# Output projections with activations as stationary operand, and sums turned by VectorE and transfers

## The chip, the cores and the metric

One NeuronCore of one Trainium2 chip runs the whole program. The metric is the device time of one execution in microseconds. Engines are PE (TensorE), PEld (its weight loads), DVE (VectorE), ACT (ScalarE), POOL (GpSimd) and SP (SyncE, which issues nearly all transfers).

## The reference

The program is a trunk of two decoder layers over 256 tokens of width 2048, in float32:

```python
h = x
for i in range(2):
    xn = rms_norm(h, norm_mix[i])
    mix = hgrn2_mixer(...) if i == 0 else short_conv_mixer(...)   # each ends in "@ w_out", 2048 x 2048
    h = h + mix
    h = h + conv_glu_ffn(rms_norm(h, norm_ffn[i]), ffn_w_up[i], ffn_conv[i], ffn_w_down[i])
return rms_norm(h, final_norm)
# hgrn2_mixer:   out = (rms_norm(o, out_gain) * silu(g)) @ w_out
# conv_glu_ffn:  u = causal_dwconv(xn @ w_up, conv_w); gate, val = split(u); (silu(gate) * val) @ w_down
```

`w_up` is 2048 x 11264 and `w_down` 5632 x 2048. Weights are read once each, about 460 MB.

## The kernel before

**Precision.** Each float32 operand is split into a high part (rounded to the fast format fp32r) and a low part, and a product is high*high + high*low + low*high. ACT makes the high part of a weight chunk (`split` on ACT, L463), DVE the low part (`split` on DVE, L742), PE multiplies.

**Chunks, groups, phases.** A `Phase` is one projection: `n` turns of a loop, `groups` groups per turn, each 512 output columns, `cpg` chunks per group (8 where 2048 rows are summed, 22 for the down projections). A chunk is 512 KB of weights. Four chunks are in flight (`RING`): while PE works on chunk c, SP loads later ones, and ACT and DVE split chunk c + 4 as soon as PE has finished chunk c. All engines walk the same list of steps (group g, step kk) and hang their other work on steps: `ahead` before the split of that step, `pieces` after it. Each engine's queue is in order.

**Two forms of matmul.** In the feature-stationary form (`parts` = 2) the weights are the stationary operand and h^T comes out, features on partitions. A chunk is four 128-row tiles by 256 columns, two parts make the 512 columns, and chunks are run in pairs: 8 high matmuls of 512 columns for each (L1392, both halves of the activation side by side), then 8 low ones of 256 for each (L1402). ACT copies the low sums out of PSUM for a correction (L470), or DVE adds both halves. In the token-stationary form (`parts` = 1, "wide") the activations are stationary (`wide_tokens`, L1458 to L1460): 12 matmuls of 512 columns a chunk, two token blocks on partitions, so the sums must be turned to features on partitions. PSUM has two sets (`SETS`) of accumulators: a wide group holds one set, a part of the other form holds one. PE waits on `acc_free` for a set when it begins a group or part, and the release comes from whoever has read it.

**Turning.** In the up projections and the second mixer's input projection, DVE transposes blocks of 32 x 32 out of PSUM into `turned` (`turn_group`, L874), SP stores it to `crossing` in HBM at step `STORED_AT` and fetches it permuted into `moved` at `FETCHED_AT` (L346, L353), and DVE takes it from there at step `SCALED_AT` of the group after (`scaled_moved`, L885), times the norm's root `rs`. In the first down projection ACT copies the sums to SBUF (L640), PE turns them with eight 128 x 128 transposes into `side` (`turn_sums`, L1368) after the first chunk of the next group, and DVE adds them to h from there.

**Around the change.** `HGRN_OUT` and `SC_OUT` are the two output projections, two loop turns of two groups, feature-stationary. At the end of a group or part DVE adds the sums to h (`h_ready`), ACT makes the high part of the next normed input and the squares (`residual`), and DVE the low part and the sum of squares (`normed`). After them comes an up projection (`UP0`, `UP1`), whose first group needs a free set and chunks already split. The order of chunks in a group is written out in `Phase.steps`.

## Time and profile before

| | |
|---|---|
| time, median of 3 runs | 2300.13 us (2299.28 to 2300.26) |
| profiled execution, its time | 2299.77 us |
| its span, first to last instruction | 2297.9 us |
| busy: PE, DVE, ACT | 99%, 74%, 46% |
| first output projection, PE | 405.5 to 497.8 us |
| first down projection, PE | 977.0 to 1219.1 us |
| second output projection, PE | 1482.6 to 1571.7 us |

Matmuls overlap, so busy time of PE is not a sum of costs: what a matmul costs is the distance of its start from the next one's. A row of the timeline is its start, its length, the engine and line, output from inputs, the shape and how many were merged; in brackets is the idle time before it and what ended that.

### The profile page before, as it was taken

The page shows a single profiled execution, that of the slowest core. Times are in us where ns is not written, and L with a number is a line of the kernel's source. Part 1 is how long each engine was busy: PE and PEld are TensorE (multiplying, and loading weights), DVE is VectorE, ACT ScalarE, POOL GpSimd, SP SyncE. Part 2 cuts the span into 40 slices and gives each one's busy share as a digit, 9 for nine tenths or more (in the row PEclk, how much of TensorE's full clock was granted, in tenths as well). Part 3 has the DMA queues.
Part 4 walks back from the last instruction along what each step waited for, and adds up shares of the span by engine and source line. Part 5 has one row for each costly group of instructions (what it writes and reads, how often), then busy time and mean ns, then how long its engine had stood idle before and what let it go on. Part 6 is the DMA issues. An engine that isn't in the chain of part 4 may idle for free.

```text
span 2297.9 us, 33410 instructions
## 1 busy us (share of the span) xinstructions
PE 2285.5 (99%) x11110; PEld 1916.0 (83%) x11110; DVE 1694.5 (74%) x2132; ACT 1049.6 (46%) x1089; POOL 2.8 (0%) x9
## 2 busy tenths in 40 slices
PE   9999999999999999999999999999999999999998
PEld 8888888888888888888888888888888888888887
DVE  7979788877878888865556676766878878876544
ACT  7444444454444454444444333444444444444443
POOL 0000000000000000000000000000000000000000
PEclk9999999999999999999999999999999999999999
DMA  7555555558888888875667888666888888887664
GB/s 247 166 174 160 179 164 166 183 189 236 242 245 233 244 243 240 242 214 188 191 191 208 243 238 245 202 193 197 248 242 240 242 244 236 241 249 219 220 192 155
DMA packets 389733, 493.55 MB, mean 215 GB/s; under 512 B 18704, under 2 KB 223888, under 8 KB 389520
## 3 DMA queue, kind: packets, MB, share of 16 engines
q1 hardware_dynamic: 388640, 490.01, 71.9%
q10 hardware_dynamic: 1008, 2.43, 0.3%
q8 instruction: 52, 0.85, 0.2%
q14 instruction: 33, 0.27, 0.0%
HBM read 459.85 MB, written 30.41 MB: 213 GB/s over the span
## 4 chain that ended last, share of the span: by engine, by line
PE 89%; DVE 6%; issue 3%; DMA 1%; ACT 1%; DVEq 0%; SPq 0%; ACTq 0%
PE acc L1459 24%; PE acc L1458 24%; PE acc L1460 24%; PE acc L1392 11%; PE acc L1402 6%; DVE w_parts L742 1%; DVE a_diag L1062 1%; DVE fpre L1047 1%; DMA raw<-in_hgrn_w_in 1%; DVE kl L1029 1%; PE side L1563 0%; DVE ql L1023 0%; ACT w_parts L463 0%; DVE ta L778 0%; DVE ta L769 0%
## 5 line engine op out<-in xcount | busy, mean ns | idle before, releaser
L742 DVE TENSOR_TENSOR w_parts<-raw,w_parts 128x1024 fp32r<-128x1024 f32 x816 | 992.8, 1224 | 551.8 <-ACT w_parts L463 425.6
L463 ACT ACTIVATE w_parts<-raw 128x1024 fp32r<-128x1024 f32 x815 | 860.1, 1059 | 1061.0 <-PE acc L1460 827.7
L1458 PE MATMUL acc<-w_parts,xn 128*128 128x512 f32 x1728 | 673.3, 390 | 0.0
L1460 PE MATMUL acc<-w_parts,xn 128*128 128x512 f32 x1728 | 672.6, 389 | 0.0
L1459 PE MATMUL acc<-w_parts,xn 128*128 128x512 f32 x1728 | 672.6, 389 | 0.0
L1458 PEld LDWEIGHTS acc<-w_parts,xn 128*128 128x128 f32 x1728 | 324.4, 188 | 67.5
L1460 PEld LDWEIGHTS acc<-w_parts,xn 128*128 128x128 f32 x1728 | 324.4, 188 | 67.2
L1459 PEld LDWEIGHTS acc<-w_parts,xn 128*128 128x128 f32 x1728 | 324.4, 188 | 66.9
L1458 PE MATMUL acc<-w_parts,act 128*128 128x512 f32 x704 | 274.3, 390 | 0.0
L1460 PE MATMUL acc<-w_parts,act 128*128 128x512 f32 x704 | 274.0, 389 | 0.0
L1459 PE MATMUL acc<-w_parts,act 128*128 128x512 f32 x704 | 274.0, 389 | 0.0
L1392 PE MATMUL acc<-xn,w_parts 128*128 128x512 f32 x896 | 216.0, 392 | 1.8 <-DVE xn L798 0.8
L1392 PEld LDWEIGHTS acc<-xn,w_parts 128*128 128x128 f32 x896 | 164.5, 188 | 35.2 <-DVE xn L798 1.4
L1459 PEld LDWEIGHTS acc<-w_parts,act 128*128 128x128 f32 x704 | 132.2, 188 | 27.4
L1460 PEld LDWEIGHTS acc<-w_parts,act 128*128 128x128 f32 x704 | 132.2, 188 | 27.4
L1458 PEld LDWEIGHTS acc<-w_parts,act 128*128 128x128 f32 x704 | 132.2, 188 | 27.2
L1392 PE MATMUL acc<-act,w_parts 128*128 128x512 f32 x512 | 122.7, 392 | 0.0
L1402 PEld LDWEIGHTS acc<-xn,w_parts 128*128 128x128 f32 x896 | 114.3, 191 | 4.8 <-DVE w_parts L742 0.4
L1402 PE MATMUL acc<-xn,w_parts 128*128 128x256 f32 x896 | 118.3, 284 | 0.0
L1392 PEld LDWEIGHTS acc<-act,w_parts 128*128 128x128 f32 x512 | 94.1, 188 | 18.2
L898 DVE SCALAR_TENSOR_TENSOR tb<-pad,par,tb 128x256 f32<-128x256 f32 x200 | 83.3, 478 | 0.0
L874 DVE STREAM_TRANSPOSE turned<-acc 128x512 f32<-128x512 f32 x108 | 71.0, 695 | 9.1 <-DVE tb L896 3.8
(157 smaller groups left out, 1223.0 us busy)
## 6 DMA issues: line engine op xcount, KB each, us to landing
raw<-in_ffn_w_up SPq DMA_DIRECT2D x352, 512.0 KB, 4.4
raw<-in_ffn_w_down SPq DMA_DIRECT2D x176, 512.0 KB, 4.6
raw<-in_hgrn_w_in SPq DMA_DIRECT2D x127, 512.0 KB, 3.8
raw<-in_sc_w_in SPq DMA_DIRECT2D x96, 512.0 KB, 4.6
crossing<-turned SPq DMA_DIRECT2D x54, 512.0 KB, 3.8
moved<-crossing SPq DMA_DIRECT2D x216, 128.0 KB, 4.5
raw<-in_hgrn_w_out SPq DMA_DIRECT2D x32, 512.0 KB, 4.0
raw<-in_sc_w_out SPq DMA_DIRECT2D x32, 512.0 KB, 4.7
```

The lines of the kernel that those rows point to most:

```text
L463: nc.scalar.activation(w_parts[:, c % RING, :, 0, :], raw[:, c % RING], ACT.Copy).then_inc(hi_ready, 1)
L742: v.tensor_tensor(w_parts[:, c % RING, :, 1, :], raw[:, c % RING], w_parts[:, c % RING, :, 0, :].bitcast(F32), ALU.subtract).then_inc(lo_r ...
L874: o = v.transpose(turned[:, :, b, :], acc[:, a % SETS, b, :].rearrange("p (j q f) -> p q j f", q=4, f=QUARTER))
L898: o = v.scalar_tensor_tensor(out=dst[:, j, :], in0=src, scalar=w, in1=dst[:, j, :], op0=ALU.mult, op1=ALU.add)
L1029: o = v.tensor_tensor(k_to[:, :, :, b], keys(kh, b, n), keys(suf, b, n), ALU.mult)
L1047: mark(v.tensor_tensor(pre[:, :, 1], pre[:, :, 1], pre[:, :, 0, n - 1:n].to_broadcast(shape), ALU.mult))
L1062: o = v.copy_predicated(a_diag[:].rearrange("p j b (w z n) -> p j (b w) z n", z=2, n=n)[:, :, :, 1], mask[:, None].to_broadcast([P, TG, P ...
L1392: o = mm(to[:, j, :], w[:, q, 0, j * P:(j + 1) * P], src[:, k * KW + q, :, :].rearrange("p n t -> p (n t)"), start=begin and q == 0, stop= ...
L1402: o = mm(to[:, j, T:], w[:, q, 1, j * P:(j + 1) * P], src[:, k * KW + q, 0, :], start=False, stop=end and q == KW - 1, skip_group_check=True)
L1458: mm(bank, x_hi, hi, start=begin and q == 0, stop=False)
L1459: low = mm(bank, x_hi, lo, start=False, stop=False)
L1460: high = mm(bank, x_lo, hi, start=False, stop=end and q == KC - 1)
```

## The change

The output projections become two phases each: three wide groups in one loop turn (`HGRN_OUT`, `SC_OUT`), then one feature-stationary group (`HGRN_LAST`, `SC_OUT_LAST`) in which chunks of the two parts alternate. Sums of a wide group are turned by DVE at its last step, cross through HBM, and are added at step 4 of the next group; ACT makes high parts and squares at step 5, DVE the low parts at step 6 (`ADDED_AT`, `SQUARED_AT`, `NORMED_AT`). In the first down projection three of four groups take the same way, with `pad` and `tb` as buffers in place of `turned` and `moved`; the last is turned by PE as before. The first down projection's sums are stored in two transfers instead of one. Set numbers are counted over the whole program where they were counted per phase.

```diff
         if self.wide(g):
             order = [(0, k) for k in range(self.cpg)]
-        elif first and g == 0 and self is HGRN_OUT:
-            order = [(0, 0), (0, 1), (1, 0), (1, 1), (0, 2), (1, 2), (0, 3), (1, 3)]
+        elif self.groups == 1:
+            order = [(0, 0), (1, 0), (0, 1), (1, 1), (0, 2), (1, 2), (0, 3), (1, 3)]
...
-HGRN_OUT = Phase(HGRN_IN, 2, 2, DT)
-UP0 = Phase(HGRN_OUT, 11, 2, DT, scales=2, corrects=False, parts=1)
+HGRN_OUT = Phase(HGRN_IN, 1, 3, DT, scales=3, corrects=False, parts=1)
+HGRN_LAST = Phase(HGRN_OUT, 1, 1, DT)
+UP0 = Phase(HGRN_LAST, 11, 2, DT, scales=2, corrects=False, parts=1)
 DOWN0 = Phase(UP0, 2, 2, FT, corrects=False, parts=1)
 SC_IN = Phase(DOWN0, 1, 10, DT, scales=10, corrects=False, parts=1)
 SC_LAST = Phase(SC_IN, 1, 2, DT, scales=2)
-SC_OUT = Phase(SC_LAST, 2, 2, DT, corrects=False)
-UP1 = Phase(SC_OUT, 11, 2, DT, scales=2, corrects=False, parts=1)
+SC_OUT = Phase(SC_LAST, 1, 3, DT, corrects=False, parts=1)
+SC_OUT_LAST = Phase(SC_OUT, 1, 1, DT, corrects=False)
+UP1 = Phase(SC_OUT_LAST, 11, 2, DT, scales=2, corrects=False, parts=1)
...
+ADDED_AT, SQUARED_AT, NORMED_AT = 4, 5, 6
...
+        turned_sums = pad[:, :, TAPS - 1:].rearrange("p q (b n) -> p q b n", b=T // P)
+        moved_sums = tb[:].rearrange("p j t -> p (j t)").rearrange("p (b a n) -> p b a n", b=T // P, a=4)
...
+            def fetch(to):
+
                 for q in range(4):
...
-                    sp.dma_start(moved[q * QUARTER:(q + 1) * QUARTER].rearrange("f b a n -> f (b a) n"),
+                    sp.dma_start(to[q * QUARTER:(q + 1) * QUARTER].rearrange("f b a n -> f (b a) n"),
                                  crossing[q].rearrange("b (a f) n -> f (b a) n", f=QUARTER)).then_inc(moved_in, 16)
+
+            def cross_sums(n, kk):
+
+                if n and kk == STORED_AT:
+                    sp.wait_ge(turned_ready, turned_groups[DOWN0] + n)
+                    for b in range(T // P):
+                        sp.dma_start(crossing[:, b].rearrange("q p n -> p q n"), turned_sums[:, :, b]) \
+                            .then_inc(sums_stored, 16)
+                if n and kk == FETCHED_AT:
+                    sp.wait_ge(sums_stored, 16 * (T // P) * n)
+                    fetch(moved_sums)
...
+            def cross_next(phase, g, kk):
+
+                if kk == STORED_AT and 0 < g <= phase.groups:
+                    store_turned(0, phase, g - 1)
+                if kk == FETCHED_AT - phase.cpg and 1 < g <= phase.groups + 1:
+                    fetch_moved(0, phase, g - 2)
...
+            stream(HGRN_OUT, hgrn_w_out[0], lambda i, g: g * GC, lambda i, first, g, kk: cross_next(HGRN_OUT, g, kk))
+            stream(HGRN_LAST, hgrn_w_out[0], lambda i, g: 3 * GC, lambda i, first, g, kk: cross_next(HGRN_OUT, 3 + g, kk))
...
+            def residual_phase(phase, last, r0, weight, rs_n=None, carry=None):
+
+                def behind(g, step):
+                    if g >= 0 and step == SQUARED_AT:
+                        for part in range(TG // TW):
+                            residual(0, r0 + g * (TG // TW), part, g * TG, weight)
...
+                def last_pieces(i, first, g, kk):
+                    behind(phase.groups - 1, kk)
+                    part, _, _, ends = last.steps(first, g)[kk]
+                    parts = range(last.parts) if rs_n is not None and kk == last.cpg - 1 else \
+                        [part] if rs_n is None and ends else []
+                    for part in parts:
+                        residual(0, r0 + phase.groups * last.parts, part, phase.groups * TG, weight)
...
-                if kk == 0 and n:
+                if kk == SQUARED_AT and n:
                     turned_residual(n - 1)
-                if kk != DOWN0.cpg - 1:
+                if (n, kk) != (DT // TG - 1, DOWN0.cpg - 1):
...
+            def add_moved(phase, g, tile, src):
+
+                dve.wait_ge(moved_in, (turned_groups[phase] + g + 1) * 4 * 16)
+                dst = h[:, tile:tile + TG, :].rearrange("p j (s t) -> p s j t", t=QUARTER)
+                v.tensor_tensor(dst, dst, src.rearrange("p b a (j t) -> p (b a) j t", j=TG), ALU.add).then_inc(h_ready, 2)
...
+                def behind(g, step):
+                    if g < 0:
+                        return
+                    tile, r, sq = g * TG, r0 + g * (TG // TW), sq0 + g * (TG // TW)
+                    if step == ADDED_AT and rs_n is not None:
+                        u = pad[:, :, TAPS - 1:]
+                        scaled_moved(0, phase, g, u)
+                        await_scaled(0, phase, g)
+                        for part in range(TG // TW):
+                            dst = h[:, tile + part * TW:tile + (part + 1) * TW, :]
+                            v.tensor_tensor(dst, dst, u[:, part * TW:(part + 1) * TW, :], ALU.add).then_inc(h_ready, 1)
+                    elif step == ADDED_AT:
+                        add_moved(phase, g, tile, moved[:])
+                    if step == NORMED_AT:
+                        dve.wait_ge(h_ready, r + TG // TW)
+                        for part in range(TG // TW):
+                            normed(0, phase, r, sq, part, tile, weight)
...
+                def turns(i, first, g, kk):
+                    if ahead:
+                        ahead(i, first, g, kk)
+                    if kk == phase.cpg - 1:
+                        turn_group(i, phase, g, turned[:])
...
+                    behind(g - 1, kk)
...
+                def last_pieces(i, first, g, kk):
+                    behind(phase.groups - 1, kk)
+                    part, _, _, ends = last.steps(first, g)[kk]
+                    tile = phase.groups * TG
...
-                        dve.wait_ge(lo_used, at(i, phase.cpi, c + 1 + RING))
+                        a = last.a0 + part
+                        c = last.c0 + kk
+                        dst = h[:, tile + part * TW:tile + (part + 1) * TW, :]
+                        dve.wait_ge(lo_used, c + 1 + RING)
                         link(v.tensor_tensor(dst, dst, acc[:, a % SETS, :, 0:T], ALU.add), i)
                         v.tensor_tensor(dst, dst, acc[:, a % SETS, :, T:], ALU.add).then_inc(h_ready, 1)
-                        dve.wait_ge(h_ready, at(i, 4, r + part + 1))
+                        dve.wait_ge(h_ready, r + part + 1)
                         v.sem_inc(acc_free, 1)
-                        normed(i, phase, r, sq, part, tile, weight)
-                phase_of(phase, pieces, ahead=ahead, into=lambda g: tb)
-
-            def turn_group(i, phase, g):
+                        normed(i, last, r, sq, part, tile, weight)
+                phase_of(phase, pieces, ahead=turns)
+                phase_of(last, last_pieces, into=lambda g: tb)
...
-                    turned_residual(n - 1)
-            phase_of(DOWN0, down)
+                r = 8 + (n - 1) * (TG // TW)
+                if n and kk == ADDED_AT:
+                    add_moved(DOWN0, n - 1, (n - 1) * TG, moved_sums)
+                if n and kk == NORMED_AT:
+                    dve.wait_ge(h_ready, r + TG // TW)
+                    for part in range(TG // TW):
+                        normed(0, DOWN0, r, r + 8, part, (n - 1) * TG, NORM_MIX + DT)
+
+            def turn_down(i, first, g, kk):
+                n = i * DOWN0.groups + g
+                if kk == DOWN0.cpg - 1 and n < DT // TG - 1:
+                    turn_group(0, DOWN0, n, turned_sums)
+            phase_of(DOWN0, down, ahead=turn_down)
...
+            phase_of(HGRN_LAST, act, act_ready, 0)
...
-            def turn_down(i, first, g, kk):
-                n = i * DOWN0.groups + g
-                if kk == 0 and n:
-                    turn_sums(n - 1)
```

## Rows read from the trace of the kernel before

**Rows 1.** The page: busy time by engine; then the chain's shares by engine.
```profile
PE 2285.5 (99%) x11110; PEld 1916.0 (83%) x11110; DVE 1694.5 (74%) x2132; ACT 1049.6 (46%) x1089; POOL 2.8 (0%) x9
...
PE 89%; DVE 6%; issue 3%; DMA 1%; ACT 1%; DVEq 0%; SPq 0%; ACTq 0%
```
**Rows 2.** Waits of PE: for whom, total us, times, longest.
```profile
PE acc L1415 <- DVE ta L769: 1.3, 1, 1.3
```
**Rows 3.** Timeline, PE, second output projection: start, us, operation, count.
```profile
1482.58 3.82 PE L1392 MATMUL acc<-act,w_parts 128*128 128x512 f32 x16
...
1493.72 3.82 PE L1392 MATMUL acc<-act,w_parts 128*128 128x512 f32 x16
1497.37 2.08 PE L1402 MATMUL acc<-act,w_parts 128*128 128x256 f32 x16
1499.28 3.82 PE L1392 MATMUL acc<-act,w_parts 128*128 128x512 f32 x16
...
1571.65 0.40 PE L1458 MATMUL acc<-w_parts,xn 128*128 128x512 f32 x1
```
**Rows 4.** Timeline, PE, first up projection: 88 matmuls from the first to the last.
```profile
529.82 0.39 PE L1459 MATMUL acc<-w_parts,xn 128*128 128x512 f32 x1
...
549.77 0.39 PE L1460 MATMUL acc<-w_parts,xn 128*128 128x512 f32 x1
```
**Rows 5.** Timeline, PE, first down projection, its second turn.
```profile
1100.34 1.03 PE L1368 MATMUL side<-ident,tb 128*128 128x128 f32 x8
...
1101.45 0.39 PE L1459 MATMUL acc<-w_parts,act 128*128 128x512 f32 x1
```
**Rows 6.** Windows: length, busy us and count of PE, PEld, DVE, ACT, POOL; PEclk, DMA.
```profile
56.00:62.00 6.00, 4.74 (x21) 3.60 (x20) 3.67 (x5) 4.02 (x5) 0.00 (x0) 1.00 0.83 262
1039.00:1220.00 181.00, 181.00 (x812) 150.14 (x811) 91.82 (x90) 79.24 (x89) 0.00 (x0) 1.00 0.61 191
```
**Rows 7.** Timelines, ACT and then DVE, first output projection, residual of one group.
```profile
437.14 0.91 ACT L514 ACTIVATE xn<-h,par 128x256 fp32r<-128x256 f32 x2 [4.24 <-DVE h L852]
...
439.80 3.89 ACT L463 ACTIVATE w_parts<-raw 128x1024 fp32r<-128x1024 f32 x4
...
438.15 0.88 DVE L798 SCALAR_TENSOR_TENSOR xn<-h,par,xn 128x256 fp32r<-128x256 f32 x2 [0.44 <-ACT xn L514]
...
440.94 4.63 DVE L742 TENSOR_TENSOR w_parts<-raw,w_parts 128x1024 fp32r<-128x1024 f32 x4
```
**Rows 8.** Waits of SyncE's queue, the store of turned sums.
```profile
SPq L346 <- DVE turned L874: 106.6, 54, 4.0
```
**Rows 9.** Timelines, ACT and then DVE, first up projection, a group's end and turn.
```profile
563.79 1.06 ACT L463 ACTIVATE w_parts<-raw 128x1024 fp32r<-128x1024 f32 x1 [1.66 <-PE acc L1460]
...
564.64 1.31 DVE L874 STREAM_TRANSPOSE turned<-acc 128x512 f32<-128x512 f32 x2 [0.19 <-DVE tb L896]
566.18 1.23 DVE L742 TENSOR_TENSOR w_parts<-raw,w_parts 128x1024 fp32r<-128x1024 f32 x1 [0.23 <-DVE turned L874]
```
**Rows 10.** Timeline, DVE: the last group's end (499 to 506); one part's sums (1500).
```profile
499.41 0.68 DVE L769 TENSOR_TENSOR tb<-acc,corr 128x512 f32<-128x512 f32 x1
...
506.28 3.49 DVE L742 TENSOR_TENSOR w_parts<-raw,w_parts 128x1024 fp32r<-128x1024 f32 x3
...
1500.87 0.68 DVE L861 TENSOR_TENSOR h<-h,acc 128x512 f32<-128x512 f32 x1
1501.59 0.69 DVE L862 TENSOR_TENSOR h<-h,acc 128x512 f32<-128x512 f32 x1
```
**Rows 11.** The page's DMA issues (KB, median us to landing); all crossing transfers.
```profile
crossing<-turned SPq DMA_DIRECT2D x54, 512.0 KB, 3.8
moved<-crossing SPq DMA_DIRECT2D x216, 128.0 KB, 4.5
...
DMA to landing us min/median/max: 2.5/4.3/9.0
```
**Rows 12.** A window after the last matmul; then the timeline of PE's warm-up.
```profile
2295.00:2298.00 3.00, 0.00 (x0) 0.00 (x0) 0.00 (x0) 0.00 (x0) 0.00 (x0) 0.50 0.58 206
...
1.08 4.09 PE L1549 MATMUL side<-ones 128*128 128x128 f32 x21 [1.08 <-POOL ones L449]
1.08 5.32 PE L1549 MATMUL side<-ones 128*128 128x128 f32 x32 [1.08 <-POOL ones L449]
```

More of the change, by code:

```diff
@@ L94, in runs @@
         single = self.parts == 1 or self is HGRN_IN and first and g == 0
-        paired = 0 if single else self.cpg - RUN if self is HGRN_OUT and first and g == 0 else end
+        paired = 0 if single else end
         return [range(k, k + RUN) for k in range(0, paired, RUN)] + [range(k, k + 1) for k in range(paired, end)]
@@ L469, in correction @@
                 act_e.wait_ge(acc_free, at(i, phase.api, phase.a0 + a + SETS))
-                nc.scalar.activation(corr[:], acc[:, a % SETS, :, T:], ACT.Copy).then_inc(corr_ready, 1)
+                nc.scalar.activation(corr[:], acc[:, (phase.a0 + a) % SETS, :, T:], ACT.Copy).then_inc(corr_ready, 1)
             def values(i, b, c):
@@ L523, in residual @@
                                      ACT.Square).then_inc(sq_ready, 1)
-            def residual_phase(phase, r0, weight, rs_n=None, carry=None):
+            def residual_phase(phase, last, r0, weight, rs_n=None, carry=None):
[3 more added lines that the diff above has]
+                            residual(0, r0 + g * (TG // TW), part, g * TG, weight)
                 def pieces(i, first, g, kk):
-                    if carry and first:
+                    if carry:
                         carry(g, kk)
-                    if rs_n is not None and first and (g, kk) == (0, RS_AT):
+                    if rs_n is not None and (g, kk) == (0, RS_AT):
                         root(rs_n)
-                    part, _, _, ends = phase.steps(first, g)[kk]
-                    tile = i * (2 * TG) + g * TG
-                    if rs_n is not None and kk == phase.cpg - 1:
-                        for part in range(phase.parts):
-                            residual(i, r0 + g * phase.parts, part, tile, weight)
-                    elif rs_n is None and ends:
-                        residual(i, r0 + g * phase.parts, part, tile, weight)
+                    behind(g - 1, kk)
[6 more added lines that the diff above has]
+                        residual(0, r0 + phase.groups * last.parts, part, phase.groups * TG, weight)
                 phase_of(phase, pieces)
+                phase_of(last, last_pieces)
             def up_phase(phase, n, rs_n):
@@ new lines, in residual_phase @@
+            def residual_phase(phase, last, r0, sq0, weight, rs_n=None, rs_stage=None, ahead=None):
+                carry = carried.pop() if carried else None
+                def behind(g, step):
[20 more added lines that the diff above has]
+                        turn_group(i, phase, g, turned[:])
@@ L843, in pieces @@
                         rms(rs_n, rs_stage)
-                    part, _, _, ends = phase.steps(first, g)[kk]
-                    tile = i * (2 * TG) + g * TG
-                    r, sq = (n0 + g * phase.parts for n0 in (r0, sq0))
-                    if rs_n is not None and kk == phase.cpg - 1:
-                        await_corrected(i, phase, g)
+                    behind(g - 1, kk)
+                def last_pieces(i, first, g, kk):
+                    behind(phase.groups - 1, kk)
+                    part, _, _, ends = last.steps(first, g)[kk]
+                    tile = phase.groups * TG
+                    r, sq = (n0 + phase.groups * last.parts for n0 in (r0, sq0))
+                    if rs_n is not None and kk == last.cpg - 1:
+                        await_corrected(i, last, g)
@@ L868, in turn_group @@
-            def turn_group(i, phase, g):
+                        normed(i, last, r, sq, part, tile, weight)
+                phase_of(phase, pieces, ahead=turns)
+                phase_of(last, last_pieces, into=lambda g: tb)
+            def turn_group(i, phase, g, to):
                 a = phase.a0 + g
@@ L945, in turns @@
                     if kk == phase.cpg - 1:
-                        turn_group(i, phase, g)
+                        turn_group(i, phase, g, turned[:])
                 def pieces(i, first, g, kk):
@@ L1259, in conv_turns @@
                 if kk == last:
[L1260 removed]
+                    turn_group(i, SC_IN, g, turned[:])
             def sc_last(i, first, g, kk):
@@ L1630, in _ @@
             phase_of(SC_OUT, act, act_ready, G + UP0.n)
+            phase_of(SC_OUT_LAST, act, act_ready, G + UP0.n)
             phase_of(UP1, xn, xn_ready, 6 * G, 2, (4, S_RS_UP1))
```

86 lines of the change are left out of this document (43 added, 43 removed).

## Prediction

> **What bounds the kernel now.** I read the shares of busy time first, then the chain of waits by engine, then the waits of TensorE (PE), then the order in time of each engine around the edited phases. PE is busy for 99% of the span, and 89% of the chain that ended last is PE [rows 1]; its clock is the upper of the two levels, 2.4 GHz (1.00 in the windows view) [rows 6]. Its longest wait for anybody is 1.3 us [rows 2]. So a matmul removed is time saved, other engines' work is free while PE need not wait for it, and each new wait of PE is time lost.
>
> **Matmul form.** In the second output projection a pair of feature-stationary chunks takes 16 matmuls of 512 columns and 16 of 256; from 1493.72 to 1499.28 that is 5.565 us, and the whole phase runs at it, 1482.58 to 1571.65 for 32 chunks, 2.783 us each [rows 3]. A token-stationary chunk is 12 matmuls of 512 columns: 88 of them from 529.82 to 549.77, 0.2267 us each, so 2.720 us a chunk [rows 4]. Columns are the same in both; the gain is 0.063 us a chunk. The change turns 24 of 32 chunks in each of two phases: 48 x 0.063 = 3.0 us saved. PE's other stages in the first projection stay; its last activation tiles are wanted at chunk 6 of group 0, as before.
>
> **Turning on TensorE.** Without the eight transposes the next matmul would begin at 1100.34; with them the second matmul after begins at 1101.45, where 1100.34 + 0.227 would be due: 0.88 us [rows 5]. Three of four go: 2.65 us saved. The 0.79 us until the first matmul alone would give 2.4, the lower end. Together the two gains are 5.7 us.
> The Trainium skill ("VectorE: DVE Perf Modes", "The three transpose paths") advises the opposite for full 128x128 blocks, TensorE, and gives 390 ns for one there; by that the saving would be 3 x 8 x 0.39 = 9.4 us. The row decides, and the advice looks at the transpose, not at the busiest engine.
>
> **Work on VectorE (DVE) and ScalarE (ACT).** Per group of the first projection DVE had 2 sums with the correction, 1 product with the root, 2 adds to h, and the normalising part (4 low parts, 2 sums of squares: 438.15 to 440.94, 2.8 us) [rows 7]. After: 2 transposes (0.695 each), 1 product of 1.22, the same adds and the same 2.8 us: 7.3 us either way. In the second it is as even. In the down projection DVE gets 2 transposes and one add of 1.22 for two adds of 0.68, +1.3 us a group, beside 22 chunks in which PE works 60 us and DVE is half idle (91.8 us busy of 181) [rows 6]; nothing is due at its steps 4 to 6, so I price it at nothing. SyncE (SP) issues for each of the 9 groups one or two stores and four fetches; a late turn holds the weight loads queued behind it, as up to 4.0 us do now [rows 8]; a weight chunk's load is issued some 7 chunks (19 us) before PE wants it, and transfers of this size land in about 4 [rows 11], so nothing either.
>
> **Bank handoff A, which I think decides.** Each last group (HGRN_LAST, SC_OUT_LAST) has the chunk order (0,0), (1,0), (0,1) ...: PE runs the eight high matmuls of part 0, 16 of which take 3.66 us, so 1.83 us, and then part 1 wants the bank set that the group just finished holds, until DVE has turned it. DVE is in order, and its step 7 (the turn) stands behind its step 6: the split of a chunk and the 2.8 us of the group before. I put the group's start at 0; chunk k ends at 2.72 x (k+1), step 7's chunk at 21.76.
> ACT splits at 0.05 us after a chunk's end (1.06 us), DVE follows (1.22, of which 1.14 until the next can begin) [rows 9]. Step 4: ACT 13.65 to 14.7, DVE split to 15.9. First projection: product 1.2 and adds 1.3, done at 18.5 (first half 17.85). ACT's step 5 squares and high parts, 2.66 us from 437.14 to 439.80 [rows 7], start with the first half: 17.9 to 20.6. Only then does ACT split for step 6, to 21.65; DVE split to 22.85, normalising to 25.65, the turn and its handoff 1.5 (564.64 to 566.18 when the next split starts [rows 9]): 27.15. PE wanted it at 21.76 + 1.83 = 23.6. Wait: 3.6 us. Second projection: one add instead of three operations, ACT 17.45 to 20.1, DVE split to 22.3, normalising to 25.1, turn 26.6: wait 3.1 us. If ACT delayed nothing, DVE would still be at the turn at 24.1, done 25.6: at least 2.0 each. The same late turn between wide groups is free, as they alternate bank sets and no split comes later than chunk 3 of the next group, due at 29.9.
>
> **Bank handoff B.** The first UP group takes the bank set of part 0, which now ends at step 6, so the cover is the low matmuls of chunk 7 alone, 0.96 us (16 take 1.91 [rows 3]). Clock from the last group's start. First projection: part 1 begins at 5.5; its pair ends at 9.2, three more pairs of 5.565 end at 25.9; lows 4 end at 19.4, lows 6 at 25.0. DVE's step 4 splits to 20.6, multiplies and adds to 23.1 (first half 22.5); ACT's residual 22.5 to 25.2, its split to 26.2, its correction (0.6) to 26.8; DVE's split to 27.4, its sum (0.7) releases the set at 28.2. PE wanted it at 25.9: wait 2.3 us, and with an ACT that never is late 1.0 (split 1.14 and sum 0.7 behind lows 6, less 0.96, and the way there). Then DVE normalises group 2 to 30.9, splits to 32.1 and does the last parts as in rows 10, where 6.9 us pass from the sum at 499.41 to the next split at 506.28: 39.0, split done 40.2; that is the fifth UP chunk, due at 28.2 + 4 x 2.72 = 39.1: 1.1 us more, at least 0. Second projection: part 1 begins at 4.9, lows 6 end at 24.4 and lows 7 at 25.4; DVE's step 4 ends at 21.3, ACT's residual at 24.0 and split at 25.0, DVE's split at 26.2, normalising at 29.0, and only behind it the two adds from PSUM (1500.87 to 1502.28 [rows 10]): release 30.5, wait 5.1 us, at least 4.5.
> Before, part 0 had ended four chunks ahead of UP, and rows 2 show no such wait. The fifth UP chunk then had 2.4 us in hand (split started 506.28, chunk due 508.7).
>
> **Sum.** Waits 3.6 + 2.3 + 1.1 + 3.1 + 5.1 = 15.2; gains 5.7; net +9.5 us. The profiled execution took 2299.77 us with a span of 2297.9, 0.36 below the median of 2300.13. 2299.77 + 9.5 = 2309.3, against the median 2309.6, which I predict. With the lower ends, 9.5 of waits, +3.8: 2303.9.
>
> **Rivals.**
> First, the handoffs are covered and only the gains are left: 2300.1 - 5.7 = 2294.4. It holds if DVE reaches the turn less than 0.3 us after the group's last chunk and part 0 is released within 0.96 us. For it: a group's turn now starts 0.9 us after its chunk, though the wait was for DVE's own work [rows 9], and PE has no waits [rows 2]. Against: 2.8 us of normalising plus a split in the 2.72 us of one chunk cannot fit.
> Second, the waits come with their least prices: 2304. For it: ACT and DVE may overlap better than my hand timeline.
> Third, more: fetched sums arrive late. A store lands after 3.8 and a fetch after 4.5 us [rows 11]; with the late turn (27.15) the store lands at 31, four fetches issue in 2.0 us and land at 37.0; step 4 of the next group wants them at 21.76 + 15.9 = 37.65. Slack 0.6 us, and landings reached 9.0 [rows 11], so A may grow by 1 to 3 us in each phase, to 2312 or 2315.
> Fourth, the clock. After the last matmul the granted clock reads 0.50 from 2295 on, that is 1.2 GHz [rows 12]; around the wait of 1.3 us it stays at 1.00 [rows 6]. My waits are longer than the one and not much longer than the other idle time. In the warm-up the first 21 matmuls took 4.09 us, all 32 took 5.32, so the other 11 took 1.2 [rows 12]: at their pace 21 take 2.35, and some 1.7 us are lost when the array starts slow. Three waits (3.1, 3.6, 5.1) at that price: +5.1, so 2314.7; the longest alone 2311.3.
> The Trainium skill ("TensorE: Matmul & The Clock Gate", "Why this matters for your kernels") says that idle gaps between bursts of matmuls bring the half-rate clock back. By that rule the fourth rival holds at least for the wait of 5.1 us.
>
> **How the numbers follow.** Forecast with full waits (2306.5 to 2313): 0.60. More (third and fourth, to 2318): 0.18. Least prices (2303 to 2306.5): 0.10. Covered: 0.12. That the matmuls do not get their 0.227 us from `act` is excluded: rows 5 show that pace from `act`. The range 2303 to 2317 leaves out the covered case and a tail. About 0.2% (4.6 us) is what a measurement tells from no change: faster 0.12, same 0.05 (the lowest of the least-price case), slower 0.83.
>
> **What would show it.** PE's waits in the profile after: four new ones, before the second run of high matmuls of each last group (3 to 4 us, ended by DVE's transpose) and before the first UP matmul (2 to 5 us, ended by a sum on DVE). The 512-column matmuls in the output projections 0.227 us apart; eight transposes left in place of 32. I am wrong if PE runs through both phase ends. If the waits stand there and the clock column dips behind them, the fourth rival holds on top.

## Result and profile after

The changed kernel takes 2318.7 us (median of 4 runs, 2316.55 to 2320.17) against 2299.93 us of the kernel before, run beside it (4 runs, 2299.28 to 2300.26): ratio 1.0083, interval 1.0068 to 1.0097. It is slower, as forecast, and by twice as much: 18.8 us where 9.5 were forecast, and 1.7 us above the range's upper end. The profiled run of it took 2316.55 us with a span of 2314.8, 16.8 us over the profiled run of the kernel before.

The page of the kernel after, busy time by engine and the shares of the chain; they answer to [rows 1]:

```profile
PE 2287.5 (99%) x10894; PEld 1909.8 (83%) x10894; DVE 1698.5 (73%) x2132; ACT 1044.8 (45%) x1077; POOL 2.8 (0%) x9
...
PE 85%; DVE 7%; issue 3%; ACT 2%; DMA 2%; DVEq 0%; SPq 0%; ACTq 0%
```

PE has 216 matmuls fewer and is busy 2.0 us more. Fewer and cheaper instructions that take longer in all: that is the first sign that some of them ran slower.

The waits of PE in the kernel after (for whom, total us, times, longest), to be held beside [rows 2], where the longest was 1.3 us:

```profile
PE acc L1484 <- DVEq L960: 8.6, 2, 4.3
PE acc L1550 <- DVEq L945: 5.2, 1, 5.2
PE acc L1550 <- DVE tb L816: 2.3, 1, 2.3
```

These are the four forecast waits, each in its place. L1484 is the high matmul of part 1, waiting for the release behind the turn (handoff A, both phases); L1550 is the first up projection matmul, waiting for part 0 of the last group (handoff B; L945 releases it in the second phase, the sum at L816 in the first).

Handoff A of the first projection, timeline of PE (start, us, operation, count, idle time before and who ended it):

```profile
473.47 0.39 PE L1552 MATMUL acc<-w_parts,act 128*128 128x512 f32 x1
473.70 1.98 PE L1484 MATMUL acc<-act,w_parts 128*128 128x512 f32 x8
479.91 3.10 PE L1484 MATMUL acc<-act,w_parts 128*128 128x512 f32 x8 [4.24 <-DVEq L960]
482.80 2.68 PE L1494 MATMUL acc<-act,w_parts 128*128 128x256 f32 x16
```

The eight high matmuls of part 0 before the wait and the eight of part 1 behind it are alike, but the first eight are 1.98 us long as a block and the others 3.10. From the start of one block to the start of the next it is 2.89 us behind the wait, where 1.83 is usual, and the 16 low matmuls that follow are slow too (2.68 us, against 2.08 in [rows 3]). The timeline of DVE for the same stretch:

```profile
474.56 1.23 DVE L789 TENSOR_TENSOR w_parts<-raw,w_parts 128x1024 fp32r<-128x1024 f32 x1 [2.28 <-ACT w_parts L502]
475.71 0.88 DVE L845 SCALAR_TENSOR_TENSOR xn<-h,par,xn 128x256 fp32r<-128x256 f32 x2
...
478.49 1.30 DVE L956 STREAM_TRANSPOSE turned<-acc 128x512 f32<-128x512 f32 x2
```

The group's last matmul is issued at 473.47. DVE then splits a chunk, normalises the group before (2.8 us), and begins the turn only 4.8 us after the group's end. Handoff B of the second phase, DVE:

```profile
1581.63 1.23 DVE L789 TENSOR_TENSOR w_parts<-raw,w_parts 128x1024 fp32r<-128x1024 f32 x1 [2.64 <-ACT w_parts L502]
1582.77 0.88 DVE L845 SCALAR_TENSOR_TENSOR xn<-h,par,xn 128x256 fp32r<-128x256 f32 x2
...
1585.56 0.68 DVE L942 TENSOR_TENSOR h<-h,acc 128x512 f32<-128x512 f32 x1
1586.27 0.69 DVE L943 TENSOR_TENSOR h<-h,acc 128x512 f32<-128x512 f32 x1
```

and PE, at the start of the up projection:

```profile
1587.07 0.80 PE L1550 MATMUL acc<-w_parts,xn 128*128 128x512 f32 x1 [5.16 <-DVEq L945]
1587.66 0.63 PE L1551 MATMUL acc<-w_parts,xn 128*128 128x512 f32 x1
1588.09 0.63 PE L1552 MATMUL acc<-w_parts,xn 128*128 128x512 f32 x1
...
1590.40 0.40 PE L1552 MATMUL acc<-w_parts,xn 128*128 128x512 f32 x1
1590.63 0.40 PE L1550 MATMUL acc<-w_parts,xn 128*128 128x512 f32 x1
```

The chain here is the forecast one: split, normalising, two sums from PSUM, release. Behind the wait the matmuls stand 0.43 us apart, then 0.23. The windows view (length, busy us and count of PE, PEld, DVE, ACT, POOL, then the clock, the DMA share and GB/s) says why; the column before the DMA share is PE's granted clock:

```profile
505.00:515.00 10.00, 10.00 (x39) 8.16 (x38) 9.48 (x17) 4.15 (x9) 0.00 (x0) 0.85 0.36 107
...
1580.00:1590.00 10.00, 4.84 (x23) 4.06 (x23) 7.36 (x13) 3.97 (x7) 0.00 (x0) 0.83 0.37 107
1590.00:1600.00 10.00, 10.00 (x45) 8.25 (x45) 6.96 (x9) 4.71 (x7) 0.00 (x0) 1.00 0.48 142
```

In 505:515 PE is busy all the time and yet does 39 matmuls in 10 us, where the full clock gives 45 (1590:1600). Around the end of each of the four waits stands such a stretch: 3.4 us at 0.50, which is 1.2 GHz. Even the wait of 2.3 us has one. In narrow windows the clock reads 0.50 from 480.75 to 484.17, 504.65 to 508.06, 1559.37 to 1562.78 and 1586.67 to 1590.09. Counted by matmuls that start too late, they cost 1.7 us (8 high and 16 low matmuls, 479.91 to 485.32), 1.7 (504.50), 1.5 (1559.86) and 1.5 (1587.07).

So the profiled run adds up to within 0.6 us. Counted from when the next matmul was due, the waits are 4.4 + 2.5 + 4.5 + 5.3 = 16.7 us. (The view above gives idle time, which is a little less.) The clock costs 1.7 + 1.7 + 1.5 + 1.5 = 6.4. Less the gains of 5.7 that the prediction put in, that is +17.4, and +16.8 was measured; the wait of 1.3 us of [rows 2] does not occur in this profile. The profiled run was the quickest of the four and its mean clock 0.996; the others had 0.994 to 0.995 and took 0.75 to 3.6 us more. By their mean clocks they spent some more time at half clock. Whether their waits were longer too is not known, since they were not profiled.

### The profile page after: what moved, and what is told of

Same layout as the page of the kernel before. It is cut to its first block, busy times and chain, and to the rows that moved or that the text cites. A ratio compares the mean times of both kernels' runs of the same rounds, so it can differ in the third digit from the quotient of the medians.

```text
span 2314.8 us, 33058 instructions
## 1 busy us (share of the span) xinstructions
PE 2287.5 (99%) x10894; PEld 1909.8 (83%) x10894; DVE 1698.5 (73%) x2132; ACT 1044.8 (45%) x1077; POOL 2.8 (0%) x9
## 4 chain that ended last, share of the span: by engine, by line
PE 85%; DVE 7%; issue 3%; ACT 2%; DMA 2%; DVEq 0%; SPq 0%; ACTq 0%
PE acc L1550 25%; PE acc L1551 25%; PE acc L1552 25%; PE acc L1484 6%; PE acc L1494 3%; DVE w_parts L789 2%; DVE a_diag L1144 1%; DVE fpre L1129 1%; ACT w_parts L502 1%; DMA raw<-in_hgrn_w_in 1%; DVE kl L1111 1%; PE side L1655 0%; DVE xn L845 0%; ACT xn L553 0%; DVE ql L1105 0%
## 5 line engine op out<-in xcount | busy, mean ns | idle before, releaser
L1550 PE MATMUL acc<-w_parts,xn 128*128 128x512 f32 x1728 | 675.3, 391 | 7.5 <-DVEq L945 5.2
L1550 PEld LDWEIGHTS acc<-w_parts,xn 128*128 128x128 f32 x1728 | 325.3, 188 | 75.5 <-DVEq L945 5.4
L1550 PE MATMUL acc<-w_parts,act 128*128 128x512 f32 x896 | 349.4, 390 | 0.0
L1552 PE MATMUL acc<-w_parts,act 128*128 128x512 f32 x896 | 349.0, 390 | 0.0
L1551 PE MATMUL acc<-w_parts,act 128*128 128x512 f32 x896 | 349.0, 390 | 0.0
L1484 PE MATMUL acc<-xn,w_parts 128*128 128x512 f32 x896 | 216.0, 393 | 1.8 <-DVE xn L845 1.0
L1552 PEld LDWEIGHTS acc<-w_parts,act 128*128 128x128 f32 x896 | 168.3, 188 | 35.0
L1551 PEld LDWEIGHTS acc<-w_parts,act 128*128 128x128 f32 x896 | 168.3, 188 | 34.8
L1550 PEld LDWEIGHTS acc<-w_parts,act 128*128 128x128 f32 x896 | 168.3, 188 | 34.4
L1484 PEld LDWEIGHTS acc<-xn,w_parts 128*128 128x128 f32 x896 | 164.7, 188 | 34.9 <-DVE xn L845 1.6
L956 DVE STREAM_TRANSPOSE turned<-acc 128x512 f32<-128x512 f32 x120 | 78.8, 695 | 9.5 <-DVE tb L978 3.9
L980 DVE SCALAR_TENSOR_TENSOR ta<-pad,par,ta 128x256 f32<-128x256 f32 x176 | 73.3, 478 | 0.0
L967 DVE TENSOR_TENSOR pad<-moved,rs 128x1024 f32<-128x1024 f32 x50 | 60.9, 1218 | 0.4 <-DMA moved<-crossing 0.4
```

Source lines behind the costliest of these rows:

```text
L956: o = v.transpose(to[:, :, b, :], acc[:, a % SETS, b, :].rearrange("p (j q f) -> p q j f", q=4, f=QUARTER))
L967: v.tensor_tensor(dst.rearrange("p j (s t) -> p s j t", t=QUARTER), moved[:].rearrange("p b a (j t) -> p (b a) j t", j=TG), rs[:, 0:T].rea ...
L980: o = v.scalar_tensor_tensor(out=dst[:, j, :], in0=src, scalar=w, in1=dst[:, j, :], op0=ALU.mult, op1=ALU.add)
L1484: o = mm(to[:, j, :], w[:, q, 0, j * P:(j + 1) * P], src[:, k * KW + q, :, :].rearrange("p n t -> p (n t)"), start=begin and q == 0, stop= ...
L1550: mm(bank, x_hi, hi, start=begin and q == 0, stop=False)
L1551: low = mm(bank, x_hi, lo, start=False, stop=False)
```

## Experiments

My theory after the result (theory 1 in the expectations below; the rivals' numbers are explained where they occur): all of the loss is PE's idle time at the two handoffs, plus a stretch at half clock that each idle time brings. Its rivals: the slow matmuls behind the waits have another cause (transfers, contention), and filling the idle time changes nothing; the turn is late because transfers are late, not because of DVE's order; the down projection carries a part of the loss; and a mended handoff only shows the next late thing.

**e1_busy: the idle time filled.** Before each of the four waits PE does extra matmuls into a spare bank, whose results nobody reads; the waits themselves stay.

```
+            n, s = {HGRN_LAST: (18, S_RS_UP0), SC_OUT_LAST: (18, S_RS_UP1), UP0: (9, S_RS_UP0),
+                    UP1: (21, S_RS_UP1)}.get(phase, (0, 0))
...
+            for _ in range(n):
+                mm(side[:, s % STAGES, 0:2 * T], src[:, 0, 0, 0:P], w_parts[:, c % RING, 0:2, 0, :], start=True, stop=True)
```

> The changed kernel, with idle time of PE filled: before each of the four waits for a bank set PE does matmuls of 512 columns whose results nobody reads (18, 18, 9 and 21 of them, 0.227 us each, about as long as the wait they stand in). Theory 1 (the waits cost 16.4 us and the lowered clock behind them another 5.7): the clock stays up, the waits stay as long in total, 2318.7 - 5.7 = 2313, between 2311.5 and 2314.5, and no matmul 0.43 us from the next. Theory 2 (the clock column is a by-product, all of the loss is waits and late transfers): 2318.7 or a little more.

Measured 2313.15 us (2311.67 to 2316.5), ratio 1.0060 (1.0046 to 1.0074): 5.5 us less than the changed kernel, with more work on PE. Its PE timeline at handoff A of the first phase:

```profile
475.14 4.24 PE L1583 MATMUL side<-w_parts,act 128*128 128x512 f32 x18
481.48 2.71 PE L1484 MATMUL acc<-act,w_parts 128*128 128x512 f32 x8 [2.10 <-DVEq L960]
```

In this run the turn came late and 2.1 us of idle time were left; behind them stands the only low stretch between the first matmul and the last. The other three handoffs have neither a wait above 0.8 us nor a low stretch. The releases did not come earlier than in the changed kernel. At B they came as late as there (in both kernels PE goes on 4.4 and 7.2 us behind the start of the last low matmuls), and at A 1.9 and 0.5 us later than there, counted from the group's end. What went is the idle time of PE. The clock's part is therefore caused by the idle time, and worth 5.5 us. One small wait is new, with the clock up, and it will matter below:

```profile
PE acc L1550 <- DVE w_parts L789: 0.5, 1, 0.5
```

**e2_cover7 and e9_cover5: more matmuls before part 1 wants its banks.** The order of the last group's chunks alone:

```
-            order = [(0, 0), (1, 0), (0, 1), (1, 1), (0, 2), (1, 2), (0, 3), (1, 3)]
+            order = [(0, 0), (0, 1), (0, 2), (1, 0), (1, 1), (1, 2), (0, 3), (1, 3)]   # e2_cover7
+            order = [(0, 0), (0, 1), (1, 0), (1, 1), (0, 2), (1, 2), (0, 3), (1, 3)]   # e9_cover5
```

> The changed kernel with the chunk order (0,0) (0,1) (0,2) (1,0) (1,1) (1,2) (0,3) (1,3) in the last groups: 7.4 us of matmuls instead of 1.8 before part 1 wants the turned group's bank set. Theory 1 (bank handoff): both waits of 4.4 and 4.5 us and the slow clock behind them (1.1 and 1.5) go, 2318.7 - 11.4 = 2307.3, within 1.5; the waits before the up projections stay at 2.3 and 5.2 us. Theory 3 (DVE and ACT have too much to do around the last groups, whatever the order): the waits move to the up projections' start, which grow by as much, 2316 to 2319.

> The changed kernel with the chunk order (0,0) (0,1) (1,0) (1,1) (0,2) (1,2) (0,3) (1,3): 5.6 us of matmuls before part 1 wants the turned group's bank set, between the 1.8 of the changed kernel and the 7.4 tried before. Theory 1: the release comes 6.2 us after the group's end (1.83 + 4.35), so 0.6 us of wait twice and no dip there, 2307.3 + 1.2 = 2308.5, within 1.5. Theory 3: as the kernel with 7.4 us of cover, whose profile had longer waits before the up projections: 2308 to 2315, with those waits above 4 us.

Measured 2307.97 us (2305.89 to 2314.71), ratio 1.0033 (1.0021 to 1.0046), and 2308.06 (2306.72 to 2310.33), ratio 1.0042 (1.0028 to 1.0055). Both take 10.6 to 10.7 us off the changed kernel, and both leave handoff B. The waits of PE in e9_cover5:

```profile
PE acc L1550 <- DVEq L945: 6.4, 1, 6.4
PE acc L1550 <- DVE tb L816: 2.5, 1, 2.5
PE acc L1484 <- DVEq L960: 1.4, 2, 1.2
```

Handoff A is down from 8.6 us to 1.4 by cover alone, while the turn itself is about as late as before: it starts 4.5 and 5.5 us behind the group's end, against 4.8 and 4.9 in the changed kernel. So a late release costs PE only what the matmuls in front of the next writer do not cover. The wait at B of the second phase grew, from 5.2 to 6.4 us: PE arrives there earlier, and the release did not move as much. So the waits at B did not stay at 2.3 and 5.2 us as theory 1 had it, though both times lie in its ranges; 2308.06 lies in theory 3's range as well. In the profiled run of e2_cover7, its longest (2314.71, the next is 2309.1), B took 4.9 and 8.5 us. ACT's timeline of that run shows what was late there:

```profile
1565.83 1.06 ACT L502 ACTIVATE w_parts<-raw 128x1024 fp32r<-128x1024 f32 x1 [5.13 <-DMA raw<-in_sc_w_out]
...
1573.74 1.06 ACT L502 ACTIVATE w_parts<-raw 128x1024 fp32r<-128x1024 f32 x1 [3.27 <-DMA raw<-in_ffn_w_up]
```

It waits for weight loads, which the prediction had priced at nothing.

**e3_early: part 0 of the second phase released first.** Its sums are added and its banks set free before the third group is normalised, not behind that.

```
-                    behind(phase.groups - 1, kk)
+                    if rs_n is not None or kk != NORMED_AT:
+                        behind(phase.groups - 1, kk)
...
+                    if rs_n is None and kk == NORMED_AT:
+                        behind(phase.groups - 1, NORMED_AT)
```

> The changed kernel, and in SC_OUT_LAST alone DVE adds part 0's sums from PSUM and releases the set before it normalises the third group (2.8 us), not behind it. Theory 1 (release behind the normalising): the wait before the second up projection falls from 5.2 to 2.4 us; with the clock still dipping 2318.7 - 2.8 = 2315.9, down to 2314.4 if it stays up. Theory 3 (total work of DVE): no change, 2318.7.

Measured 2315.57 us (2313.09 to 2317.51), ratio 1.0068 (1.0054 to 1.0082). The waits of PE:

```profile
PE acc L1490 <- DVEq L966: 10.1, 2, 5.1
PE acc L1556 <- DVEq L945: 2.4, 1, 2.4
```

B of the second phase falls from 5.2 to 2.4 us, which is the 2.8 us of normalising that no longer stand before the release. (A is at 10.1 us in this profiled run, 1.5 more than in that of the changed kernel. In the first phase, where the two kernels are the same, it is 5.1 against 4.2, so A differs by as much from one execution to another.) The order of DVE sets that wait, not a transfer.

**e4_down: the down projection alone.** The kernel before, with only the three groups of DOWN0 turned on DVE and sent through the crossing transfers.

```
-HGRN_OUT = Phase(HGRN_IN, 1, 3, DT, scales=3, corrects=False, parts=1)
-HGRN_LAST = Phase(HGRN_OUT, 1, 1, DT)
+HGRN_OUT = Phase(HGRN_IN, 2, 2, DT)
...
-SC_OUT = Phase(SC_LAST, 1, 3, DT, corrects=False, parts=1)
-SC_OUT_LAST = Phase(SC_OUT, 1, 1, DT, corrects=False)
+SC_OUT = Phase(SC_LAST, 2, 2, DT, corrects=False)
```

> The kernel before with the change of the first down projection alone: three of its four groups turned by DVE and transfers. Theory 1: 24 transposes of PE go, 2299.9 - 2.65 = 2297.3, within 0.5, and PE has no wait in that phase. Theory 2 (the new transfers hold the weight loads): 2300 or more.

Measured 2296.55 us (2296.01 to 2297.0), ratio 0.9987 (0.9978 to 0.9996). That part of the change gains 3.05 us where 2.65 were forecast. DVE's timeline shows the turn and the add in the idle time that the prediction had named as cover; the split between them starts 0.2 us after the turn:

```profile
1094.38 1.23 DVE L769 TENSOR_TENSOR w_parts<-raw,w_parts 128x1024 fp32r<-128x1024 f32 x1 [1.49 <-ACT w_parts L492]
1095.94 1.31 DVE L907 STREAM_TRANSPOSE pad<-acc 128x512 f32<-128x512 f32 x2 [0.34 <-PE acc L1503]
1097.49 1.23 DVE L769 TENSOR_TENSOR w_parts<-raw,w_parts 128x1024 fp32r<-128x1024 f32 x1 [0.23 <-DVE pad L907]
...
1111.84 1.22 DVE L899 TENSOR_TENSOR h<-h,tb 128x1024 f32<-128x1024 f32 x1
```

**e5_spread: normalising kept out of the turn's way.** The first two wide groups are normalised one part at a time in steps 1 and 2 of the group after next, where DVE is free; only the third still stands at step 6.

```
+LATER_AT = [1, 2]
...
-                    if step == NORMED_AT:
+                    if step == NORMED_AT and g == phase.groups - 1:
...
+                    if 0 <= g < phase.groups - 1 and step in LATER_AT:
...
+                        normed(0, phase, r, sq, LATER_AT.index(step), g * TG, weight)
```

> The changed kernel with the normalising part of the first two wide groups moved on DVE from step 6 of the next group to steps 1 and 2 of the one after, so that nothing but a split stands ahead of the third group's turn at its step 7. The order in the last groups stays (cover 1.8 us). Theory 1 (the turn is late because of the 2.8 us in front of it): the turn starts within 0.2 us of the group's last matmul, both waits of 4.4 us fall under 0.3, the weights are no longer late either, and what is left is the waits of 2.3 and 5.2 us before the up projections: 2307.3, within 1. Theory 4 (weight loads or fetched sums come late through traffic, not through DVE): ACT still waits 2 to 5 us for weights and the up projections' waits are 5 and 8 us as in the profile of the kernel with 7.4 us of cover: 2310 to 2314.

Measured 2306.91 us (2305.52 to 2307.79), ratio 1.0032 (1.0021 to 1.0043). The waits of PE:

```profile
PE acc L1560 <- DVEq L955: 5.2, 1, 5.2
PE acc L1560 <- DVE tb L817: 2.3, 1, 2.3
PE acc L1494 <- DVEq L970: 1.9, 1, 1.9
```

The time is as expected, but not all of the reason. A keeps 1.9 us in the first phase, nearly none in the second, and no low clock follows it: in 476:481 and 481:486, on both sides of that wait's end, the granted clock is 1.00. The turn starts 2.5 us behind the group's end in the first phase and 0.7 in the second, not within 0.2. In the second phase ACT waits for no weights before the turn; in the first it still does, as theory 4 had it, three times up to 3.4 us:

```profile
470.38 1.06 ACT L503 ACTIVATE w_parts<-raw 128x1024 fp32r<-128x1024 f32 x1 [3.39 <-DMA raw<-in_hgrn_w_out]
```

The eight weight loads issued there (453 to 473 us) took 3.7 to 9.3 us from issue to landing, 7.4 in the median. Up to this turn e7_both and e8_put_off differ from this kernel only in the order in which the last group's weights are loaded and split, and from each other in nothing; they show one such wait (2.7 us) and none. So this part of A differs from one execution to another, with transfers that land late; what makes them late is not shown.

From e2_cover7, e9_cover5 and this run together: A goes either by more cover or by less work before the turn, and takes its clock stretch with it, 10.6 to 11.8 us for the two phases.

**e6_seq: the last group's parts one after the other**, so that part 0 ends four chunks ahead of the up projection, as in the kernel before; its sums in the second phase are released at step 3's end, as in e3_early.

```
-            order = [(0, 0), (1, 0), (0, 1), (1, 1), (0, 2), (1, 2), (0, 3), (1, 3)]
+            order = [(part, k) for part in range(2) for k in range(self.cpg // 2)]
```

> The changed kernel with the parts of the last groups one after the other (chunks (0,0) to (0,3), then (1,0) to (1,3)); in SC_OUT_LAST DVE adds part 0's sums at step 3 and frees its bank set there, its normalising stays at step 6. Theory 1 (both handoffs are a matter of cover: now 11.1 us at the start and four chunks at the end): no wait for a bank set, all four stalls gone; 2318.7 - 22.1 = 2296.6 or down to 2294 if no split is late for the first chunks of the up projections. Theory 3 (DVE's total work binds): waits for its splits, 4 us and more at each up projection, 2302 and more.

Measured 2303.34 us (2300.81 to 2305.92), ratio 1.0016 (1.0007 to 1.0025). No bank is waited for any more, at A or at B, but the time is 6.7 us above the 2296.6 that this alone would give, in the range of theory 3. The waits of PE name what took their place:

```profile
PE acc L1556 <- DVE w_parts L789: 6.5, 3, 3.5
```

and DVE's timeline at the end of the first phase why:

```profile
501.35 1.22 DVE L789 TENSOR_TENSOR w_parts<-raw,w_parts 128x1024 fp32r<-128x1024 f32 x1
502.48 0.68 DVE L816 TENSOR_TENSOR tb<-acc,corr 128x512 f32<-128x512 f32 x1
...
508.99 3.49 DVE L789 TENSOR_TENSOR w_parts<-raw,w_parts 128x1024 fp32r<-128x1024 f32 x3
```

Between the split at 501.35 and the next at 508.99 DVE does the last group's residual and its normalising. The weights of a further up projection chunk are split only then. This is the third of the prediction's waits, C. It did not show in the changed kernel because the low clock behind handoff B made PE 1.7 us later there: the split ended at 516.02, the fifth chunk began at 517.10, and at full speed it would have been due at 504.50 + 4 x 2.72 = 515.38, 0.6 us before the split's end. That is the new wait of e1_busy, where the clock stays up: 0.6 us from when the matmul was due. Without the wait at B, PE comes earlier still, and C grows to 3.6 us here. Theory 3 is settled by e8_put_off below.

**e7_both: e5_spread and e6_seq together.**

> Both edits of the two kernels before in one. Theory 1: no bank wait and no late split; only the two gains are left, 2299.6 - 3.0 - 2.65 = 2293.9, up to 2296.5 where a split for the fifth chunk of an up projection is late by the 1.1 us of the prediction and the clock dips. If the matmul form gains nothing, it ends at the 2296.55 of the kernel with the down projection's change alone.

Measured 2298.55 us (2296.59 to 2299.44), ratio 0.9994 (0.9985 to 1.0003), 2 us over the upper end expected. One wait is left, and PE's timeline shows it with its low stretch:

```profile
506.62 0.39 PE L1568 MATMUL acc<-w_parts,xn 128*128 128x512 f32 x1
509.49 0.76 PE L1566 MATMUL acc<-w_parts,xn 128*128 128x512 f32 x1 [2.48 <-DVE w_parts L790]
510.05 0.63 PE L1567 MATMUL acc<-w_parts,xn 128*128 128x512 f32 x1
510.47 0.63 PE L1568 MATMUL acc<-w_parts,xn 128*128 128x512 f32 x1
```

That wait is 2.64 us from when the matmul was due and costs 1.7 us of clock, and a second one takes 0.6 (idle time): 4.9 in all. Without them the run would stand at 2293.7, about where the gains alone put it (2294.4). My expectation had taken C for smaller than it is.

**e8_put_off: e7_both, with C taken away too.** The last group's normalising, in the second phase that of its part 1, is moved behind the first splits of the up projection, one part each at its steps 1 and 2; ACT's part of it goes to step 0.

```
-                        for part in range(last.parts):
-                            dve.wait_ge(h_ready, r + part + 1)
-                            normed(i, last, r, sq, part, tile, weight)
...
+                    if kk == last.cpg - 1:
+                        put_off_norms.append(lambda part: normed(0, last, r, sq, part, tile, weight))
...
+                    if first and g == 0 and kk in LATER_AT:
+                        put_off_norms[-1](LATER_AT.index(kk))
```

> The kernel with both edits, and the last group's residual put off: ACT makes its high parts and squares at step 0 of the up projection, behind that step's split (in SC_OUT_LAST only part 1's), DVE normalises both parts at steps 1 and 2 instead of before its split for the fifth up chunk. Theory 1 (what is left in 2298.55 is the late split, 2.5 and 0.7 us of wait, and one dip of the clock, 1.7): PE waits nowhere around the output projections, 2298.55 - 4.9 = 2293.7, within 0.7, below the 2296.55 of the down projection's change alone by the 3.0 of the matmul form. Theory 3 (DVE's total work binds): the wait moves to a later chunk, 2297 or more.

Measured 2294.07 us (2293.49 to 2294.6, 11 runs), ratio 0.9977 (0.9968 to 0.9986) against the kernel before: the quickest version of the case, 5.3 us under the kernel before and 24.6 under the changed one, with all parts of the change in it. DVE is busy for 1698.1 us in it and for 1698.5 in the changed kernel, so theory 3 is wrong: it is the order of DVE's work that cost time, not its amount. The longest wait of PE is 1.1 us and lies in the warm-up, and the granted clock is 1.00 where it was 0.85:

```profile
PE side L1662 <- POOL ones L489: 1.1, 1, 1.1
```

```profile
505.00:515.00 10.00, 9.82 (x43) 7.79 (x42) 7.97 (x12) 6.54 (x9) 0.00 (x0) 1.00 0.55 159
```

## Why the prediction came out as it did

The sign and the mechanism were right; the size was not, and the range missed by 1.7 us.

```
term                         forecast      profile of after     by
A, first phase               3.6           4.4                  e5, e2, e9
A, second phase              3.1           4.5                  e5, e2, e9
B, first phase               2.3           2.5                  e6
B, second phase              5.1           5.3                  e3, e6
C, fifth up chunk            1.1           0 (2.6 in e7)        e1, e7, e8
clock behind the waits       0 (rival)     6.4                  e1 (5.5)
gains                        -5.7          (-5.3)               e4, e8
```

**The step that failed is the clock.** The prediction left it out of the sum and gave it, with the late sums, 0.18. It argued that a wait of 1.3 us had left the clock at 1.00 and that 3 to 5 us "are longer than the one and not much longer than the other idle time". That is an interpolation between a row at 1.3 us and the end of the program, and the truth lay at the near end: 2.3 us of idle time is enough here. With the fourth rival's own price of 1.7 us for each wait and all four waits in place of three, the sum would have been 2309.6 + 6.8 = 2316.4. That price, taken from the warm-up, was near: the four stretches cost 1.5 to 1.7 us each. The rule of the Trainium skill ("TensorE: Matmul & The Clock Gate", "Why this matters for your kernels") that gaps between bursts bring the half-rate clock back was quoted beside that rival and not allowed to weigh. The trace agrees with it for the waits of 4.2, 4.3 and 5.2 us; the one of 2.3 us is shorter than the gaps for which it is stated, and here the measurement decides: that wait has its low stretch too.

**A was too small by 0.8 and 1.4 us.** The hand timeline let ACT split each chunk as soon as DVE's chain allowed. In the run ACT stood before the splits for its weights, here in the first phase:

```profile
463.70 1.06 ACT L502 ACTIVATE w_parts<-raw 128x1024 fp32r<-128x1024 f32 x1 [2.28 <-DMA raw<-in_hgrn_w_out]
...
469.88 1.06 ACT L502 ACTIVATE w_parts<-raw 128x1024 fp32r<-128x1024 f32 x1 [2.92 <-DMA raw<-in_hgrn_w_out]
```

The prediction let a transfer of this size land in about 4 us and priced the loads at "nothing either". The nine loads issued here from 453 to 476 us took 3.5 to 8.2 us, 6.0 in the median. In the second phase these waits go when the normalising is moved (e5_spread), so there DVE's order is part of it; in the first phase they stayed in that run, and e7_both and e8_put_off, alike up to there, have one and none, so there the landings themselves vary. No run takes the two causes apart.

**B came out to 0.2 us**, and e3_early shows that its second-phase excess is the normalising put before the release. **C** was worked out behind the wait at B, so summing the two was right. With the clock up it is there, at 0.6 us (e1_busy) for 1.1 forecast; the clock stretch that the sum left out covered it in the changed kernel. Without the wait at B it is 2.6 us and has a clock stretch of its own (e7_both).

**The gains** stand. e4_down has 3.05 us for three turns (2.65 forecast), so DVE's extra work there and the crossing transfers are hidden, as priced. The 9.4 us that the prediction set beside them, from 390 ns for one transpose, did not come. The step from e4_down to e8_put_off is 2.5 us for the form of 48 chunks (3.0 forecast), or 2.3 if each is held against the kernel before run beside it; matmuls from `act` in the token form do come 0.226 us apart (eight from 450.81 to 452.62):

```profile
450.81 0.39 PE L1551 MATMUL acc<-w_parts,act 128*128 128x512 f32 x1
...
452.62 0.39 PE L1550 MATMUL acc<-w_parts,act 128*128 128x512 f32 x1
```

**The first rival** (covered, 2294.4) was wrong for this kernel and right for the idea: e8_put_off is that case, made by order alone, at 2294.07. **The third** did not appear as such in the changed kernel: in the first phase the scaled product waits 0.38 us for its fetched sums, in the second nothing. But transfers that land late are, as read from the trace, a part of A's excess, with the weight loads in place of the sums. The range's upper end of 2317 would have held the forecast waits plus four stretches (2316.4); it had no room for A's further 2.2 us on top, nor for executions of one kernel that differ by 3.6 us.

One sum of the prediction is off without effect: DVE's work of one group, given as 7.3 us, adds up to 6.7 from its rows, before and after alike.

## What to carry to other kernels

When PE is busy 99% of the time, a change that alters which group holds which bank set is priced by the releases: write down, for each set, when the last reader is done and how many matmuls stand before the next writer; work on the releasing engine that nobody waits for (here 2.8 us of normalising) must not stand before the release. Price each new wait of PE of over 2 us with a stretch at half clock, here 1.5 to 1.7 us more, and up to 3.0 behind waits of 4.9 us and more. A gain of 5 us was in the change all along; it took another order of the last group's chunks and of three pieces of side work to get it. Mending A made the wait at B longer (e9_cover5), and mending B brought out C.

## What the hardware showed

Over the ten profiles of the changed kernel and of the experiments, every idle time of PE of 3.5 us or more within the run was followed by a stretch at 1.2 GHz (ten of ten). Of those of 2.1 to 2.5 us, seven of eight were. The eighth, 2.52 us in e9_cover5 before the first up projection matmul, was not:

```profile
498.31 0.50 PE L1550 MATMUL acc<-w_parts,xn 128*128 128x512 f32 x1 [2.52 <-DVE tb L816]
498.65 0.40 PE L1551 MATMUL acc<-w_parts,xn 128*128 128x512 f32 x1
```

Its next matmul follows after 0.34 us, where e7_both shows 0.56 and then 0.42. None of 1.9 us or less was followed by one. What decides between the cases near 2.5 us is not settled by these runs.

The clock did not always fall during the wait. In the changed kernel the first stretch began 0.8 us after PE had taken up its matmuls again (480.75, the wait ended at 479.91), and the one in e1_busy 1.3 us after; others began 0.4 to 0.5 us before the wait's end (1586.67 and 1587.07). The low time was 3.4 us behind waits of 2.1 to 5.2 us and 6.8 or 10.2 us around some of the waits from 4.9 to 8.5, a part of it within the wait. It cost about half of what lay behind the wait: 1.7 us where all 3.4 us did, 1.5 where 2.9 or 3.0 did, and 2.9 in e9_cover5, where 6.1 of 10.2 us did.
